# Attention steps with the values behind the scores, masks in pairs, index scores in groups of four units

## What is computed

```python
# index score of the sparse attention, 8 heads of 64
logits = jnp.einsum('bqhd,bsd->bqhs', qib, k_idx)
score = jnp.einsum('bqhs,bqh->bqs', jax.nn.relu(logits), wb)
_, idx = lax.top_k(score, n_sel)
# attention, heads of 64, query blocks of 128, here the forgetting one
s = jnp.einsum('bqhd,bshd->bhqs', qb, k)
s = s * scale + cb[..., None] - c[:, :, None, :]
s = jnp.where(mask, s, -jnp.inf)
p = jax.nn.softmax(s, axis=-1)
return jnp.einsum('bhqn,bshd->bqhd', p, v)
```

## Time and profile before

| | us |
|---|---|
| median of 3 runs | 2418.17 (2417.23 to 2418.5) |
| the profiled execution | 2416.57 |
| its span, first to last instruction | 2414.8 |
| mean granted TensorE clock, share of full | 0.997 |
| TensorE busy | 2371.4 (98%) |
| VectorE, ScalarE, GpSimd busy | 1034.8, 956.0, 1049.1 |
| stages that the change touches, layer 1 | index scores 50 to 100, dilated attention 127 to 225, sparse attention 225 to 284 |
| the same of layer 2 | 693 to 743, 770 to 866, 867 to 926 |
| forgetting attention | 1371 to 1461 |

### The profile page before, as it was taken

How to read it: one execution, slowest core, us unless ns; L and a number is a source line. 1 busy time by engine, 2 the same in 40 slices (tenths; PEclk the granted TensorE clock), 3 DMA queues, 4 the chain that set the end, 5 groups by cost and what they waited for, 6 DMA issues and landing times. The chain is left out here.

```text
span 2414.8 us, 29460 instructions
## 1 busy us (share of the span) xinstructions
PE 2371.4 (98%) x11832; PEld 1900.5 (79%) x11832; DVE 1034.8 (43%) x1906; ACT 956.0 (40%) x1338; POOL 1049.1 (43%) x831
## 2 busy tenths in 40 slices
PE   8999999999999999999999999999999999999997
PEld 6777688888877767888888769888889779788887
DVE  4687531121348865221126445322225768322224
ACT  5345542232343455332235455422124485322223
POOL 4435244454444253444545453443444334444442
PEclk9999999999999999999999999999999999999999
DMA  5223122323222121323233212322332312322331
GB/s 167 76 62 106 36 96 96 105 88 105 83 93 88 53 97 53 105 88 105 89 104 101 87 36 71 105 84 90 105 98 95 105 53 88 105 90 85 105 105 53
DMA packets 139624, 214.40 MB, mean 89 GB/s; under 512 B 7776, under 2 KB 66272, under 8 KB 139232
## 3 DMA queue, kind: packets, MB, share of 16 engines
q1 hardware_dynamic: 139488, 212.51, 27.1%
HBM read 208.30 MB, written 2.10 MB: 87 GB/s over the span
## 5 line engine op out<-in xcount | busy, mean ns | idle before, releaser
L273 POOL TENSOR_TENSOR w_lo<-raw,w_hi 128x512 fp32r<-128x512 f32 (+1 forms) x776 | 992.3, 1313 | 1312.4 <-ACT w_hi L263 1312.1
L311 PE MATMUL ps<-h_hi,w_hi 128*128 128x512 f32 x1696 | 683.2, 403 | 11.3 <-POOL w_lo L273 11.1
L311 PE MATMUL ps<-h_hi,w_lo 128*128 128x512 f32 x1696 | 663.6, 391 | 0.0
L311 PE MATMUL ps<-h_lo,w_hi 128*128 128x512 f32 x1696 | 663.2, 391 | 0.0
L263 ACT ACTIVATE w_hi<-raw 128x2048 fp32r<-128x2048 f32 (+2 forms) x205 | 362.3, 1781 | 569.1 <-PE ps L311 443.8
L311 PE MATMUL ps<-hid_hi,w_hi 128*128 128x512 f32 x992 | 391.7, 395 | 4.7 <-DVE hid_lo L946 2.7
L311 PEld LDWEIGHTS ps<-h_hi,w_hi 128*128 128x128 f32 x1696 | 318.6, 188 | 92.7 <-issue 18.3
L311 PE MATMUL ps<-hid_hi,w_lo 128*128 128x512 f32 x992 | 387.2, 390 | 0.0
L311 PE MATMUL ps<-hid_lo,w_hi 128*128 128x512 f32 x992 | 387.0, 390 | 0.0
L311 PEld LDWEIGHTS ps<-h_lo,w_hi 128*128 128x128 f32 x1696 | 318.4, 188 | 70.1 <-issue 5.6
L311 PEld LDWEIGHTS ps<-h_hi,w_lo 128*128 128x128 f32 x1696 | 318.0, 187 | 70.5 <-issue 0.4
(11 more groups left out here) (302 smaller groups left out, 2800.8 us busy)
## 6 DMA issues: line engine op xcount, KB each, us to landing
raw<-in_w_up SPq DMA_DIRECT2D x32, 1024.0 KB, 5.3
raw<-in_w_down SPq DMA_DIRECT2D x32, 1024.0 KB, 5.0
raw<-in_ffn_w_gate SPq DMA_DIRECT2D x44, 512.0 KB, 4.0
raw<-in_ffn_w_up SPq DMA_DIRECT2D x44, 512.0 KB, 5.0
raw<-in_w_in SPq DMA_DIRECT2D x20, 1024.0 KB, 5.0
raw<-in_ffn_w_down SPq DMA_DIRECT2D x20, 1024.0 KB, 5.0
raw<-in_w_out SPq DMA_DIRECT2D x8, 1024.0 KB, 5.4
raw<-in_ev_w_in SPq DMA_DIRECT2D x8, 1024.0 KB, 5.3
```

The source lines that it names most:

```text
L273: pool.tensor_tensor(w_lo[slot.buf][:, k, 0:slot.width], raw[r][:, k, 0:slot.width], w_hi[slot.buf][:, k, 0:slot.width].bitcast(F32), ALU. ...
L311: mm = pe.matmul(o, lh, rh, start=first and q == 0, stop=last and q == 2, skip_group_check=True)
```

## The change

Only the order changes; every matmul stays, and 64 negations of one column are merged away.

- The values of units i-4 and i-3 now stand in the even step i directly behind the scores of units i and i+1, in place of units i-5 and i-4 in the odd step. Block ends come one step earlier (`OUT, HIGH, LOW` = 4, 5, 6), and an attention has one step less. The output projections' `Pace` is shortened so that they end with it; `dil_pace` still has 36 steps.
- In the even step VectorE makes the masks of units i and i+1, then one negation of two columns; ScalarE's order is as before, apart from the block ends.
- Index scores go in groups of four units, twelve matmuls in a row, behind the tiles of four units; a group waits for the relu of all units before it.

```diff
-            SUMS, TURN_SUMS, OUT, HIGH, LOW = 2, 3, 5, 6, 7
+            SUMS, TURN_SUMS, OUT, HIGH, LOW = 2, 3, 4, 5, 6
...
-                return len(self.units) + self.VAL + 3
+                return len(self.units) + self.LOW
...
-                    u = i - self.VAL - 1
+                    u = i - self.VAL
                     if 0 <= u < n and u % 2 == 0:
                         self.values(pe, u)
...
-                dve.wait_ge(*at("s_masked", self.u0 + i + 1))
-                sg["nmax"].by(dve.tensor_scalar(sn[:, i:i + 1], sx[:, i:i + 1], -SCALE, None, ALU.mult))
+                dve.wait_ge(*at("s_masked", self.u0 + i + 2))
+                sg["nmax"].by(dve.tensor_scalar(sn[:, i:i + 2], sx[:, i:i + 2], -SCALE, None, ALU.mult), 2)
...
-                    if i < n:
+                    if i < n and i % 2 == 0:
                         self.mask(dve, i)
+                        self.mask(dve, i + 1)
                         self.negate(dve, i)
...
-            dil_pace = Pace(3 * 32, 0, dil.steps() - 3)
-            out_a, out_b0, out_b1 = Pace(16, 0, 3), Pace(8, 12, 6), Pace(8, 18, 5)
+            dil_pace = Pace(3 * 32, 0, dil.steps() - 2)
+            out_a, out_b0, out_b1 = Pace(16, 0, 3), Pace(8, 12, 6), Pace(8, 18, 4)
...
-                for i in range(0, len(units), 2):
+                for i in range(0, len(units), 4):
                     qb, h = units[i]
-                    idx_pace.emit(i, tiles)
-                    idx_pace.emit(i + 1, tiles)
+                    for u in range(i, i + 4):
+                        idx_pace.emit(u, tiles)
                     if i == 0:
                         pe.wait_ge(*at("q_low", 4))
                         pe.wait_ge(*at("kk_low", 1))
-                    if i == 2:
                         pe.wait_ge(*at("col_ready", 1))
                         pe.wait_ge(sems["ln_done"], pl.n_ckv.i + 1)
-                    if i >= 4:
-                        pe.wait_ge(*at("idx_relu", i - 2))
+                    else:
+                        pe.wait_ge(*at("idx_relu", i))
...
-                    for n, (a_q, a_k) in enumerate(((q_hi, kk_hi), (q_hi, kk_lo), (q_lo, kk_hi))):
-                        for e in range(2):
-                            rows = slice(HD * e, HD * e + HD)
-                            mm = pe.matmul(ps[:, (i + e) % 4, 0:w], a_q[rows, h // 2, q], a_k[rows, 0:w],
-                                           start=n == 0, stop=n == 2)
-                            if n == 2:
-                                sg["idx_ready"].by(mm)
+                    for d in range(0, 4, 2):
+                        for n, (a_q, a_k) in enumerate(((q_hi, kk_hi), (q_hi, kk_lo), (q_lo, kk_hi))):
+                            for e in range(2):
+                                rows = slice(HD * e, HD * e + HD)
+                                mm = pe.matmul(ps[:, d + e, 0:w], a_q[rows, (h + d) // 2, q], a_k[rows, 0:w],
+                                               start=n == 0, stop=n == 2)
+                                if n == 2:
+                                    sg["idx_ready"].by(mm)
...
-                out_a, out_b = Pace(16, 25, 7), Pace(16, 32, 7)
+                out_a, out_b = Pace(16, 25, 7), Pace(16, 32, 6)
```

## The result

The changed kernel takes 2434.45 us (median of 4 runs, 2432.91 to 2438.57) against 2418.34 for the kernel before: 1.0072 times as long, 95% interval 1.0056 to 1.0088. The forecast was 2420.7 with a range up to 2427.0, so it is 14 us too low and the time lies outside the range.

What follows compares the result with a forecast made beforehand. TensorE's own queue was taken as the bound, busy 2371.4 of 2414.8 us. Terms -11.5 + 6.3 + 10.5 - 5.1 + 1.4 + 0.9 = +2.5 on 2418.2 gave 2420.7 us, range 2413.5 to 2427.

Steps and rivals of the forecast that it cites:

- The 64 negations that go are worth nothing: VectorE has room.: In the attention stages, dropping 64 negations on VectorE was given no effect on the time.
- the rule on the shared ports: Index scores: two-SBUF-input VectorE and SBUF-reading GpSimd instructions exclude each other; up to 0.9 us per layer.
- Uncovered transposes: After groups of eight units, two transposes with no values between: 0.57 us each at 11 places, +6.3 us.
- A mask more ahead of the exponential: Attention stages: both masks precede one negation, so even units' exponentials and the next odd transposes come later; +10.5 us.
- The place that rests on the earlier trace: Dilated attention, unit 13's transpose: slack 0.04, a mask of 0.69 more makes it 0.66 us late.
- Index scores: Index stage: 12 fewer visits save 4.8 us; waits for the last unit's evacuation add 1.4.
- a loss of 0.9 that VectorE's lateness was to carry into the dilated attention: VectorE comes about 1.5 us late from the index stage, costing dilated attention's first units 0.45 per layer.
- Sparse attention: Sparse attention stages: all terms together make each layer's stage +0.4 us longer; masks are 2.5 over two layers.
- The gain at its end: End of sparse attention: chain product, copy, subtraction come a step earlier, shortening the output projection's wait; -1.16 net per layer.
- The slower one: Dilated attention: paired masks also wait behind top-k search instructions on VectorE; 5.0 us more, 2425.7, chance 0.30.
- The faster one: Attention stages: exponentials early enough, masks cost nothing, 2410.2; with the transposes' 6.3 hidden too, 2403.9; chance 0.17.

Runs made afterwards that it cites:

- the run with two negations: Changed kernel with two one-column negations in place of each two-column one, masks still in pairs: 2423.70 us.
- the run with masks apart: Changed kernel with mask and one-column negation in every step, as before the change; moved values and index scores in fours stay: 2414.16 us.
- the accumulating form: Changed kernel with its two-column negation also summing its output into a column that nobody reads: 2424.13 us.
- fastest kernel: Changed kernel with masks and negations in every step, sparse attention's values in the odd step, and projection tiles ahead of the transpose of unit 8j+1: 2404.37 us.

## Why the prediction was wrong

**The step that failed** is the sentence "The 64 negations that go are worth nothing: VectorE has room." I counted the instructions that went and not what became of those that stayed: a negation of two columns is another thing than one of one column. Three runs show it: taken away from the changed kernel it gives 10.8 us, by another form 10.3, and put into the kernel before it costs 10.2. One to two of the 10.8 seem to go by way of the clock: among the few executions with the same mean granted clock (0.996 and 0.997) the changed kernel takes 8.6 to 9.4 more than the run with two negations. The range had no room for it, and no rival named it. I had even weighed the rule on the shared ports, for the index scores, where it decides at most 0.9 us per layer, and not for the one instruction whose form the change alters. On the list of edits "merged, fewer" looked like the only one without a price.

**Uncovered transposes: right.** 0.68 from start to start was worked out, 0.68 is what 159.60 to 160.28 shows, and tiles between them gave 4.9 us at nine places where 5.1 was expected.

**A mask more ahead of the exponential: right in mechanism and in the sum, and the sum in part by luck.** 10.5 forecast, 9.5 measured as the difference of the runs with masks in pairs and apart. By stages of the profiled executions that difference is 2.28 and 1.41 in the dilated attentions (forecast 2.1 each and 0.7 in one of them), 0.25 and 0.26 in the sparse ones (forecast 1.2 each) and 7.0 in the forgetting attention (forecast 3.1). In the sparse attention the longer waits for retention's products take the mask in: they fall from 2.6 to 1.7 us in all. In the forgetting attention the run with masks in pairs has the granted clock at 0.50 from 1431.7 to 1441.9 us, up to 5.1 us of full speed, and the run with masks apart keeps 1.00; that belongs to no term of the sum. The place that rests on the earlier trace rows has in the run with two negations a wait of 0.50 before the transpose of unit 13 and the start 0.90 behind the tile before it instead of 0.23, so 0.67 late against 0.66 worked out.

**Index scores: right in mechanism and size.** 4.8 saved and 1.4 given back made 3.4; alone they gave 3.0, and in the changed kernel's trace 3.2. The tile that waits for VectorE's evacuation waits 0.31 (83.44 us of the changed kernel), less than my 0.6; a loss of 0.9 that VectorE's lateness was to carry into the dilated attention doesn't exist in the run of the index part alone (0.00 and -0.05).

**Sparse attention: wrong by 3.7 us in the sum of both layers** in the run with two negations (+2.96 and +1.66 against 0.44 each). The term gave the transposes and copies their due and took retention for filler. With masks apart the two stages grow by 4.1 us, where the forecast's terms without the masks' 2.5 give -1.6. So the values' move was mis-sized by 5.7, and the masks' term, which is nearly absent in this stage (0.5 for 2.5), hid 2.0 of it. Of the 4.1, 1.6 are longer waits for retention's products, 1.3 the lower clock in layer 1, and about 1 the uncovered transposes, which the forecast had. The gain at its end was there (with masks apart TensorE's start of the output projection's last part came 1.64 nearer in layer 1), but the last values waited 1.69 for the last copy first.

**The sum, mended**: +2.5 as forecast, +10.8 for the negation and +3.7 for the sparse attention are +17.0; measured are +16.1. The rest of the sum was within a microsecond or two, with errors of both signs that cancel, as the stages of the masks' term show: the run with two negations took 2423.7, near the forecast of 2420.7 plus 3.7.

**The rivals.** The slower one (masks lumped behind the search) has no place of its own in the traces: with short negations units 3, 7, 11 and 23 of the first dilated attention don't wait, and unit 9 waits only for the copy that the forecast had. Its 2425.7 lies near the 2423.7 of that run, but not for its reason. The faster one is out, but a kernel as fast as its lower end, 2404, exists: the cost of the masks and of the uncovered transposes could be left out by leaving these parts out, not by their being hidden.

## What to carry to other kernels

When two small instructions are merged, compare the form and not the count: a plain VectorE `tensor_scalar` in SBUF with one element per partition never waited for GpSimd here, one with two did, up to 1.2 us, and it stood at the head of a chain through three engines. Before moving a block of matmuls, ask what it covers on both sides: the same values hid a copy in one stage and another engine's products in another, and one reordering rule for three stages had two signs. A change of several parts is worth taking apart: its index part and its values part gain where they fit, and one line hid it.

## What was not expected of the hardware

**The granted clock falls where TensorE has stood still in a stage that is thin anyway.** The tail of the dilated attention in the changed kernel, the transposes of units 27 and 29 on TensorE's timeline:

```profile
212.63 0.41 PE L852 MATMUL ps<-tab,p 128*128 128x128 f32 x2 [1.68 <-ACT p L961]
...
219.48 0.87 PE L852 MATMUL ps<-tab,p 128*128 128x128 f32 x3 [2.70 <-ACT p L961]
```

The windows there (stretch and length, busy time and number of instructions of TensorE's matmuls, its weight loads, VectorE, ScalarE and GpSimd, then the granted clock as a share of full, DMA share and GB/s), changed kernel:

```profile
212.00:220.00 8.00, 4.67 (x37) 3.81 (x38) 7.19 (x17) 5.59 (x13) 8.00 (x7) 0.93 0.00 0
218.80:222.20 3.40, 2.72 (x12) 2.53 (x12) 2.48 (x6) 1.78 (x6) 3.40 (x4) 0.50 0.02 5
220.00:226.00 6.00, 5.98 (x46) 5.30 (x44) 4.03 (x8) 1.78 (x4) 6.00 (x6) 0.81 0.01 3
868.00:874.00 6.00, 5.97 (x45) 5.41 (x44) 4.01 (x8) 1.69 (x3) 6.00 (x6) 0.77 0.02 4
```

and before:

```profile
212.00:220.00 8.00, 5.68 (x54) 5.04 (x54) 7.69 (x19) 5.17 (x9) 8.00 (x7) 1.00 0.01 2
220.00:226.00 6.00, 6.00 (x60) 5.30 (x56) 3.43 (x7) 1.90 (x4) 6.00 (x5) 1.00 0.00 0
```

Before, this stage kept 1.00, 2.4 GHz, all through. In the changed kernel the clock goes to 0.50, 1.2 GHz, at 218.8, inside the wait of 2.70 us that ends at 219.48, and is back at 1.00 from 222.2: 0.07 x 8 + 0.19 x 6 = 1.7 us of full speed missing in layer 1, and 0.23 x 6 = 1.4 in the window of layer 2. This is an upper bound of the price, since TensorE idles in a part of the stretch. That a wait can cost more than its length is shown by the kernel with masks apart, whose two sparse attentions have the same waits: with 0.50 from 274.8 to 278.3 behind them the stage grew by 1.3 us more.

The clock doesn't fall in every kernel with such waits: in the run with two negations the dilated attentions kept 1.00 in the profiled execution and grew by -0.13 and +0.85, while the accumulating form, equal in the median, was at 0.81 and 0.72 there and grew by 2.42 and 3.39. Nor is it new with the change: the kernel before is at 0.50 from 1426.0 to 1432.8 in the forgetting attention, around the end of its wait of 2.57, and the run with two negations has such stretches in its first sparse attention (278.0 to 281.4) and in the forgetting one. The fastest kernel has none before its last microseconds.

The scatter of the times goes with it. Of the ten executions of the run with two negations the two shortest (2420.7) have a mean granted clock of 0.998 and 0.999 and the longest (2427.4) 0.995; of the seven of the accumulating form the shortest (2422.8) has 0.998 and the longest (2429.4) 0.995. The fastest kernel's five lie between 2403.8 and 2405.7, all at 0.998 or 0.999. What makes one execution keep the clock and another not is open.

**The two-column negation also takes the longest while GpSimd works on weights**: it ends with GpSimd's instruction and not after a fixed time, up to 1.21 us where one of GpSimd's takes about 1.27.
